# Where the first visit's last two gate/up chunks land, and when the second visit's are fetched

## The chip, the cores and the metric

The kernel runs on one core of a Trainium2 chip. The metric is the device time of one execution in microseconds. The engines are PE (matmuls), DVE, ACT, POOL and SP; SP only issues transfers. Sixteen DMA engines move the data. Transfers issued by SP go through one hardware queue (q1 in the trace), those issued by POOL through another (q0).

## The reference, cut to what matters

One decoder block on 512 tokens of width 1024: a gated DeltaNet group and a convolution group side by side, an output projection with a residual, and then a mixture of experts:

```python
logits = (xt @ w_router + b_router)
top_val, top_idx = lax.top_k(logits, TOP_K)          # 4 of 32 experts
gates = jax.nn.softmax(top_val, axis=-1)
...
hid = x_blk @ w_gate_up[e] + b_gate_up[e]            # 1024 -> 2 x 1024
gate, up = hid[:, :D_FF], hid[:, D_FF:]
gate = jnp.minimum(gate, SWIGLU_LIMIT)
up = jnp.clip(up, -SWIGLU_LIMIT, SWIGLU_LIMIT)
glu = gate * jax.nn.sigmoid(SWIGLU_ALPHA * gate)
return ((up + 1.0) * glu) @ w_down[e] + b_down[e]    # 1024 -> 1024
```

All in float32. Each expert has 8 MB of gate/up weights and 4 MB of down weights, and all 32 are read once.

## The kernel before

The first part (projections, convolutions, the delta rule, output projection) ends with the residual rows `x2`. Then each 128-row tile `t` of four is normed into `xn[:, t % 2, :]`, which lies in `convbuf`, and POOL writes it to `xn_rows` in DRAM (line 543, semaphores `xn_out`). In parallel PE transposes the rows, ACT and DVE copy them as `xnT` into `qkbuf`, and PE forms the logits from it (line 1743, `lgT_done`). Neither buffer is used after that.

The experts are worked through in 32 *visits*, one for each expert, with up to 128 of its tokens in up to four groups of 32. A visit needs:

- its tokens' rows, fetched by POOL with four indirect transfers (*gathers*, line 557) out of `xn_rows` into `wq`. Before the first gather POOL waits for all `xn_out` and for the row numbers (`idx_ready`, made by DVE at line 1352) and copies the numbers (line 552). DVE transposes the rows (`xt_turn`, line 1332, `xt_ready`);
- eight *gate/up chunks* of 1 MB each, one in each slot of `ring`, fetched by SP (line 378, `slot_in[0..7]`);
- four *down chunks* of 1 MB in `dslots` (line 385, `slot_in[8..11]`).

PE's `gate_up(i)` takes the ring slots in pairs (line 1854); after each chunk it raises `gu_used`. Then it runs `down(i - 1)` (line 1890, `d_used`). SP works through one list in order. Visit 0's chunks 0 to 3 are issued after the last projection tile; ring slots 4 to 7 hold the output projection's weights until `op_done` is T, so chunks 4 and 5 follow this, and chunks 6 and 7 also wait for the last normed row:

```python
            for c in range(KC):
                if c == 4:
                    sp.wait_ge(op_done, T)
                if c == 6:
                    sp.wait_ge(xn_ready, T)
                gate_up(0, c)
```

Then come down chunks 0 and 1, a wait for visit 0's gathers, down chunks 2 and 3, a wait for `route_ready`, and visit 1's chunks, each after a wait for `gu_used` of the same slot in visit 0. From visit 2 on a loop issues eight gate/up chunks of visit i and four down chunks of visit i - 1, each when PE has used what the slot held.

Between the router and visit 0, DVE and PE add the experts' gated down biases to `x2` (`routed_bias`, line 1841, and lines 1389 and 1390, `acc_ready`); POOL writes the sums to `acc_rows` (line 590), to which each visit's results are later added by indirect transfers (*scatters*, line 562). PE starts `gate_up(0)` when `xt_ready` is 1 and `acc_ready` is T.

Of the kernel before, what the change touches and what calls it, by code (L numbers as in the profile page):

```python
# [38 lines left out]
def block_kernel(nc, x, attn_norm_w, w_in, gdn_conv_w, gdn_a_log, gdn_dt_bias, gdn_norm_w, cf_dw_w, cf_dw_b,  # L39
                 cf_ln_w, cf_ln_b, w_out, ffn_norm_w, w_router, b_router, w_gate_up, b_gate_up, w_down,  # L40
                 b_down, final_norm_w, out):
    _, SEQ, D = x.shape
# [7 lines left out]
    T = SEQ // P  # L50
    KC = D // P
# [8 lines left out]
    SLOT = 2 * D  # L60
# [10 lines left out]
    with ExitStack() as ctx:  # L71
# [3 lines left out]
        def sem(name):  # L75
            return ctx.enter_context(nc.semaphore(name))


        ring = sb("ring", 8 * SLOT)
# [4 lines left out]
        qkbuf = sb("qkbuf", 2 * 2 * SEQ)  # L84
# [3 lines left out]
        convbuf = sb("convbuf", 2 * (SEQ + CONV - 1) + 2 * SEQ)  # L88
# [14 lines left out]
        def view(t, start, *dims):  # L103
            n = 1
            for d in dims:
                n *= d
            v = t[:, start:start + n]
            names = "abcd"[:len(dims)]
            if len(dims) > 1:
                v = v.rearrange(f"p ({' '.join(names)}) -> p {' '.join(names)}",  # L110
                                **{names[i]: dims[i] for i in range(1, len(dims))})
            return v
# [47 lines left out]
        def take(*dims):  # L160
            n = 1
            for d in dims:
# [53 lines left out]
        finw = rows[:, D:2 * D]  # L216
        fin = view(hbuf, 0, T, D)

        bank = [ctx.enter_context(nc.psum_tensor(f"bank{i}", [P, 512], F32)) for i in range(8)]

        xn_dram = nc.dram_tensor("xn_rows", [NR_ROWS, D], F32, kind="Internal").ap()
# [7 lines left out]
        slot_in = [sem(f"slot_in{i}") for i in range(12)]  # L229
        param_in, gate_in, bias_in, late_in, wr_in = (sem(n) for n in  # L230
                                                      ("param_in", "gate_in", "bias_in", "late_in", "wr_in"))
        fin_in = [sem(f"fin_in{t}") for t in range(T)]
        acc_out, last_out = sem("acc_out"), sem("last_out")
        xn_out = [sem(f"xn_out{i}") for i in range(2)]
# [29 lines left out]
        op_done, x2_ready, rstd2_ready, xn_ready, xn_turned, xnT_ready = (sem(n) for n in (  # L264
            "op_done", "x2_ready", "rstd2_ready", "xn_ready", "xn_turned", "xnT_ready"))
        lgT_done, lgT_copied, lg_done, mx_ready, ex_ready, gate_ready = (sem(n) for n in (
            "lgT_done", "lgT_copied", "lg_done", "mx_ready", "ex_ready", "gate_ready"))
# [82 lines left out]
        @block.sync  # L350
        def _(sp):
            sp.dma_start(xr[:, 0, :], x2d[0:P, :]).then_inc(x_in[0], 16)

            for i, v in enumerate((cf_dw_b, cf_ln_w, cf_ln_b)):
                sp.dma_start(prow[TAPS + i:TAPS + i + 1, :], v).then_inc(param_in, 16)
            sp.dma_start(prow[34:46, :], gdn_conv_w[0].rearrange("w (s c) -> (w s) c", s=3)).then_inc(param_in, 16)
            sp.dma_start(prow[46:48, :], attn_norm_w.rearrange("o (r c) -> (o r) c", r=2)).then_inc(param_in, 16)
            sp.dma_start(prow[48:50, :], ffn_norm_w.rearrange("o (r c) -> (o r) c", r=2)).then_inc(param_in, 16)
            for t in range(1, T):
                sp.dma_start(xr[:, t, :], x2d[t * P:(t + 1) * P, :]).then_inc(x_in[t], 16)  # L360
            for u in range(NU):
                if u >= 8:
                    sp.wait_ge(proj_done, LAST_TILE[u - 8] + 1)
                if u < NU - 2:
                    src = win[:, :, UNITS[u]:UNITS[u] + 256]
                else:
                    c = 4 * (u - NU + 2)
                    src = win[:, c:c + 4, OFF_Z:OFF_Z + QK]
                sp.dma_start(unit_ap(u), src).then_inc(slot_in[u % 8], 16)
            for i in range(4):  # L370
                sp.wait_ge(proj_done, LAST_TILE[4 + i] + 1)
                sp.dma_start(view(ring, (4 + i) * SLOT, 2, D), wout[:, 2 * i:2 * i + 2, :]).then_inc(
                    slot_in[4 + i], 16)

            def gate_up(i, c):
                e = i % E
                src = w_gate_up[0, e].rearrange("(p c) n -> p c n", c=KC)[:, c, :]
                sp.dma_start(view(ring, c * SLOT, SLOT), src).then_inc(slot_in[c], 16)  # L378

            def down_rows(e, u):  # L380
                return w_down[0, e].rearrange("(p c) n -> p c n", c=KC)[:, 2 * u:2 * u + 2, :]

            def down(i, u):
                e = i % E
                sp.dma_start(view(dslots, u * SLOT, 2, D), down_rows(e, u)).then_inc(slot_in[8 + u], 16)

            sp.wait_ge(proj_done, NT)
            for t in range(T):
                sp.dma_start(x2[:, t, :], x2d[t * P:(t + 1) * P, :]).then_inc(xres_in[t], 16)
            for c in range(KC):  # L390
                if c == 4:
                    sp.wait_ge(op_done, T)
                if c == 6:
                    sp.wait_ge(xn_ready, T)
                gate_up(0, c)
            for u in range(4):
                if u == 2:
                    sp.wait_ge(gathered, 16 * GROUPS)
                down(0, u)
            sp.wait_ge(route_ready, 1)  # L400
            m = visits_less_two(sp)
            for c in range(KC):
                sp.wait_ge(gu_used, c + 1)
                gate_up(1, c)
            with sp.Fori(2, m + 2) as i:
                for c in range(KC):
                    sp.wait_ge(gu_used, (i - 1) * KC + c + 1)
                    gate_up(i, c)
                for u in range(4):
                    sp.wait_ge(d_used, (i - 1) * 4 + u + 1)  # L410
                    down(i - 1, u)

            for u in range(4):
                sp.wait_ge(gu_used, m * KC + (KC + 2 * u + 2))
                sp.dma_start(view(ring, u * SLOT, 2, D), down_rows(E - 1, u)).then_inc(slot_in[u], 16)

            sp.wait_ge(scattered, m * (16 * GROUPS) + 32 * GROUPS)
            sp.wait_ge(acc_out, 16 * T)
            for t in range(T):
                sp.dma_start(fin[:, t, :], acc_dram[t * P:(t + 1) * P, :]).then_inc(fin_in[t], 16)  # L420
            for t in range(T):
                sp.wait_ge(fin_ready, t + 1)
                sp.dma_start(out2d[t * P:(t + 1) * P, :], fin[:, t, :]).then_inc(last_out, 16)
            sp.wait_ge(last_out, 16 * T)
# [1047 lines left out]
        def _(pe):  # L1472
# [4 lines left out]
            for j in range(CT):  # L1477
                ins = TR(view(bank[3], 0, CT, 64)[:, j, 0:50], prow[0:50, j * P:(j + 1) * P], ident[0:50, 0:50])
            ins.then_inc(params_turned, 1)
            for t in range(T):  # L1480
# [4 lines left out]
                for c in range(KC):  # L1485
                    ins = TR(bank[c][:, t * P:(t + 1) * P], xr[:, t, c * P:(c + 1) * P], ident)
# [5 lines left out]
            for r in range(2):  # L1492
                for j in range(4):
                    c = 4 * r + j
# [134 lines left out]
            for s in range(NT):  # L1629
                h, steps = gdn_of(s)  # L1630
# [179 lines left out]
            for u in range(T):  # L1810
                ins = M(bank[7][:, 0:E], ones16, Msk[:, u, :], start=(u == 0), stop=(u == T - 1))
# [36 lines left out]
            m = visits_less_two(pe)  # L1848
            pe.sem_inc(d_used, 4)

            def gu_mm(c, g):
                w = view(ring, c * SLOT, 2, D)
                for j in range(4):
                    ins = M(bank[g][GROUP * j:GROUP * (j + 1), :], xT[:, g, c * GROUP:(c + 1) * GROUP],  # L1854
                            w[:, :, j * QD:(j + 1) * QD], start=(c == 0), stop=(c == KC - 1))
                return ins

            def gate_up(i, first=False):

                tokens = tokens_left(pe, i)  # L1860
                for c0 in range(0, KC, 2):
                    pe.wait_ge(slot_in[c0], i * 16 + 48)
                    pe.wait_ge(slot_in[c0 + 1], i * 16 + 48)
                    with pe.If(tokens > 2 * GROUP):
                        for c in (c0, c0 + 1):
                            gu_mm(c, 2)
                        with pe.If(tokens > 3 * GROUP):
                            for c in (c0, c0 + 1):
                                gu_mm(c, 3)
                    for c in (c0, c0 + 1):  # L1870
                        for g in range(2):
                            ins = gu_mm(c, g)
                        ins.then_inc(gu_used, 1)
                    if first and c0 == 0:
                        pe.wait_ge(idx_ready, 1)
                        idx_mm(1, 2 * T + 1)
                    if first and c0 == 6:
                        pe.wait_ge(idx_ready, 2)
                        idx_mm(2, 3 * T + 2)
                    if not first and c0 == 4:  # L1880
                        pe.wait_ge(idx_ready, i + 2)
                        idx_mm((i + 2) % E, (i + 3) * (T + 1) - 1)
# [87 lines left out]
```

## Time and profile before

| | |
|---|---|
| median of 3 runs | 1496.38 us (1495.18 to 1496.44) |
| the profiled execution | 1496.78 us, span 1495.0 us |
| busy: PE, DVE, POOL, ACT | 1285.7, 704.2, 379.5, 202.9 us |
| granted TensorE clock, mean | 0.947 |
| DMA traffic | 451.08 MB, mean 302 GB/s |

The span runs from the first to the last instruction of the core. A busy share is an average over stages, so it does not tell what a change in one stage is worth. In the windows view each line is a stretch: its length, then the busy time of each engine, then the granted clock (1.00 is 2.4 GHz, 0.50 is 1.2 GHz), the share of time for which the 16 DMA engines were busy, and GB/s. In the views of instructions the first two numbers are start and duration in us, SPq stands for an issue by SP, and a bracket gives the engine's idle time before it and what ended it. An arrow reads "written from".

### The profile page before, as it was taken

To read this page: it belongs to the slowest core of one execution; us is meant where nothing else is said; L and a number is where in the kernel's file an instruction comes from. 1 tells how busy PE (TensorE), PEld (TensorE's weight loads), DVE (VectorE), ACT (ScalarE), POOL (GpSimd) and SP (SyncE) were. 2 spreads that over 40 slices of the span, in tenths; PEclk is the share of its full clock that TensorE was granted. 3 is DMA by queue.
4 is the path that set the end of the run, shared out by engine and by line. 5 is a ranking of instruction groups with operands and counts; after the bars stand their busy time and mean duration, and the time that the engine had idled before them with its cause. 6 is when DMAs were issued, how large, how long until landed. Compare 5 with 4: busy or idle time off the path is not lost.

```text
span 1495.0 us, 31945 instructions
## 1 busy us (share of the span) xinstructions
PE 1285.7 (86%) x12386; PEld 563.6 (38%) x12387; DVE 704.2 (47%) x1335; ACT 202.9 (14%) x372; POOL 379.5 (25%) x434
## 2 busy tenths in 40 slices
PE   6997989879878999989989899878888887889982
PEld 3444555555422344333423333323323332233331
DVE  2888888653533345342533325433334443333441
ACT  3123323131300001000100000100000010000012
POOL 4001111020221224322342222333222233222233
PEclk9999999979969999999999999999999999999996
DMA  9221000210368999999999999999999999999984
GB/s 305 67 72 64 1 29 1 112 60 18 117 269 300 391 410 407 403 413 410 411 405 411 409 411 413 408 412 410 409 416 411 409 414 404 401 406 411 410 298 143
DMA packets 93589, 451.08 MB, mean 302 GB/s; under 512 B 18265, under 2 KB 36853, under 8 KB 44375
## 3 DMA queue, kind: packets, MB, share of 16 engines
q1 hardware_dynamic: 70182, 427.88, 70.6%
q0 software_dynamic: 20304, 21.03, 6.1%
q10 hardware_dynamic: 3072, 1.76, 0.5%
q8 instruction: 20, 0.33, 0.1%
q14 instruction: 11, 0.08, 0.0%
HBM read 439.05 MB, written 17.17 MB: 305 GB/s over the span
## 4 chain that ended last, share of the span: by engine, by line
PE 48%; DMA 35%; DVE 10%; issue 3%; ACT 2%; SPq 1%; POOL 1%; POOLq 0%; ACTq 0%; DVEq 0%
DMA ring<-in_w_gate_up_dram 34%; PE bank L1854 24%; PE bank L1890 8%; PE bank L1548 5%; PE bank L1715 4%; DVE dslots L991 2%; DVE qkbuf L1015 1%; PE bank L1614 1%; PE bank L1543 1%; PE bank L1608 1%; DMA xn_rows<-convbuf 1%; DVE vbuf L1015 1%; PE bank L1681 1%; SPq L378 1%; PE bank L1841 0%
## 5 line engine op out<-in xcount | busy, mean ns | idle before, releaser
L1854 PE MATMUL bank<-ring,wq 128*32 128x512 f32 x5184 | 613.8, 626 | 114.2 <-DMA ring<-in_w_gate_up_dram 92.9
L1854 PEld LDWEIGHTS bank<-ring,wq 128*32 128x32 f32 x5184 | 169.2, 114 | 518.2 <-issue 517.8
L1890 PE MATMUL bank<-dslots,intra 128*32 128x256 f32 x5056 | 282.1, 379 | 3.7 <-DMA dslots<-in_w_down_dram 3.4
L1349 DVE TENSOR_REDUCE small<-bank 128x4 f32<-128x8 f32 x34 | 5.7, 167 | 472.7 <-PE bank L1821 472.7
L1890 PEld LDWEIGHTS bank<-dslots,intra 128*32 128x32 f32 x5056 | 166.4, 110 | 127.3 <-issue 28.6
L552 POOL COPY idx_in<-idx 128x4 int32 (+1 forms) x34 | 12.1, 357 | 594.6 <-DVE wq L1332 580.6
L890 ACT ACTIVATE zrows<-intra 128x1024 f32<-128x1024 f32 x32 | 33.8, 1057 | 898.6 <-DVE intra L1429 704.6
L1548 PE MATMUL bank<-hbuf,ring 128*128 128x512 f32 x320 | 147.6, 602 | 0.0
L562 POOL DMA_INDIRECT acc_rows<-rows,idx_out x83 | 133.2, 1605 | 46.5 <-POOL idx_out L552 27.4
L1409 DVE STREAM_TRANSPOSE wq<-bank 128x512 f32<-128x512 f32 x128 | 80.3, 685 | 98.9 <-PE bank L1854 98.9
L557 POOL DMA_INDIRECT wq<-xn_rows,idx_in x88 | 106.9, 1214 | 49.4 <-POOL idx_in L552 29.3
L991 DVE SCALAR_TENSOR_TENSOR dslots<-dslots,small 128x512 f32<-128x512 f32 x120 | 91.8, 765 | 2.7
L1548 PEld LDWEIGHTS bank<-hbuf,ring 128*128 128x128 f32 x320 | 58.7, 194 | 58.4 <-issue 58.4
L1332 DVE STREAM_TRANSPOSE wq<-wq 128x1024 f32<-128x1024 f32 x33 | 67.6, 2047 | 6.7 <-DMA wq<-xn_rows,idx_in 6.7
L569 POOL DMA_DIRECT2D spare<-in_gdn_dt_bias_dram x93 | 68.6, 841 | 0.1
L1715 PE MATMUL bank<-ring,dslots 128*128 128x512 f32 x128 | 59.9, 614 | 2.8 <-DVE dslots L1170 2.8
L884 ACT ACTIVATE rows<-bank,small 128x256 f32<-128x256 f32 x124 | 48.6, 475 | 60.3 <-PE bank L1890 54.9
L1441 DVE SCALAR_TENSOR_TENSOR intra<-zrows,intra 128x1024 f32<-128x1024 f32 x32 | 39.3, 1227 | 22.8 <-PE bank L1890 19.6
L1422 DVE TENSOR_TENSOR zrows<-wq,small 128x256 f32<-128x256 f32 x128 | 45.6, 419 | 0.0
L1323 DVE TENSOR_SCALAR rows<-slot_no,small 128x512 bf16<-128x512 bf16 x140 | 40.1, 350 | 10.1 <-DVE idx L1352 9.6
L1422 DVE TENSOR_TENSOR intra<-wq,small 128x256 f32<-128x256 f32 x128 | 44.5, 409 | 0.0
L491 POOL TENSOR_TENSOR sqbuf<-qkbuf 128x512 f32<-128x512 f32 x8 | 10.4, 1306 | 126.7 <-DVE qkbuf L1033 126.7
(263 smaller groups left out, 897.2 us busy)
## 6 DMA issues: line engine op xcount, KB each, us to landing
ring<-in_w_gate_up_dram SPq DMA_DIRECT2D x256, 1024.0 KB
dslots<-in_w_down_dram SPq DMA_DIRECT2D x124, 1024.0 KB
ring<-in_w_in_dram SPq DMA_DIRECT2D x12, 1024.0 KB
ring<-in_w_out_dram SPq DMA_DIRECT2D x4, 1024.0 KB
ring<-in_w_down_dram SPq DMA_DIRECT2D x4, 1024.0 KB
rows<-in_x_dram SPq DMA_DIRECT2D x4, 512.0 KB, 6.2
hbuf<-in_x_dram SPq DMA_DIRECT2D x4, 512.0 KB, 5.1
xn_rows<-convbuf POOLq DMA_DIRECT2D x4, 512.0 KB, 4.1
```

Of the source, the lines that this page charges most:

```text
L557: pool.indirect_dma_start(out=xg[:, g, :], out_offset=None, in_=xn_q, in_offset=bass.IndirectOffsetOnAxis(ap=idx_in[:, g:g + 1], axis=0), ...
L562: pool.indirect_dma_start(out=acc_q, out_offset=bass.IndirectOffsetOnAxis(ap=idx_out[:, g:g + 1], axis=0), in_=yb[:, g, :], in_offset=None ...
L569: pool.dma_start(spare[0:1, k * H:(k + 1) * H], gdn_dt_bias[0:1, :]).then_inc(done, 16)
L884: ins = A(yb[:, g, :], bank[4 + g // 2][:, (g % 2) * QD:(g % 2 + 1) * QD], ACT.Copy, scale=gates[:, bass.ds(stage * GROUPS + g, 1)])
L991: own.mark(V.scalar_tensor_tensor(out=cacc[:, j, :], in0=ubuf[:, j, k:k + SEQ], scalar=PT[:, j, k:k + 1], in1=cacc[:, j, :], op0=ALU.mult, ...
L1332: V.transpose(xT.rearrange("p g (c s) -> p g c s", c=KC), xg.rearrange("p g (r c) -> p g c r", c=KC)).then_inc(xt_ready, 1)
L1409: V.transpose(hidT[:, g, :, :].rearrange("p h (c s) -> p h c s", c=KC), bank[g][:, :].rearrange("p (h r c) -> p h c r", h=2, c=KC)).then_i ...
L1422: V.tensor_tensor(out[:, g, :].rearrange("p (b s) -> p b s", b=KC), hidT[:, g, half, :].rearrange("p (b s) -> p b s", b=KC), bias.to_broad ...
L1548: ins = M(bank_of(s)[:, :], unit_ap(u)[:, c, half * P:(half + 1) * P], hT[:, c, :], start=(c == 0), stop=(c == KC - 1))
L1715: ins = M(pair[half][:, :], lhs, w, start=(kc == 0), stop=(kc == KC - 1))
L1854: ins = M(bank[g][GROUP * j:GROUP * (j + 1), :], xT[:, g, c * GROUP:(c + 1) * GROUP], w[:, :, j * QD:(j + 1) * QD], start=(c == 0), stop=( ...
L1890: ins = M(b[GROUP * j:GROUP * (j + 1), col:col + QD], actT[:, g, c * GROUP:(c + 1) * GROUP], w[:, cc, j * QD:(j + 1) * QD], start=(c == 0 ...
```

## The change

Visit 0's chunks 6 and 7 no longer go to ring slots 6 and 7. Chunk 6 goes to `qkbuf` after `lgT_done` has reached T, chunk 7 to `convbuf` after all four `xn_rows` writes have landed. SP's waits for the writes stand ahead of chunk 7 and so also ahead of down chunks 0 and 1. Both chunks raise a semaphore of their own, `early_in`. Ring slots 6 and 7 are then free, and SP issues visit 1's chunks 6 and 7 right after `route_ready`, ahead of visit 1's chunks 0 to 5, which wait for `gu_used` as before. PE reads visit 0's chunks 6 and 7 from the two buffers and counts one landing less on `slot_in[6]` and `slot_in[7]`.

```diff
--- before.py
+++ after.py
@@ -216,6 +216,7 @@
         finw = rows[:, D:2 * D]
         fin = view(hbuf, 0, T, D)
 
+        EARLY = {6: view(qkbuf, 0, SLOT), 7: view(convbuf, 0, SLOT)}
         bank = [ctx.enter_context(nc.psum_tensor(f"bank{i}", [P, 512], F32)) for i in range(8)]
 
         xn_dram = nc.dram_tensor("xn_rows", [NR_ROWS, D], F32, kind="Internal").ap()
@@ -229,6 +230,7 @@
         slot_in = [sem(f"slot_in{i}") for i in range(12)]
         param_in, gate_in, bias_in, late_in, wr_in = (sem(n) for n in
                                                       ("param_in", "gate_in", "bias_in", "late_in", "wr_in"))
+        early_in = sem("early_in")
         fin_in = [sem(f"fin_in{t}") for t in range(T)]
         acc_out, last_out = sem("acc_out"), sem("last_out")
         xn_out = [sem(f"xn_out{i}") for i in range(2)]
@@ -372,10 +374,11 @@
                 sp.dma_start(view(ring, (4 + i) * SLOT, 2, D), wout[:, 2 * i:2 * i + 2, :]).then_inc(
                     slot_in[4 + i], 16)
 
-            def gate_up(i, c):
+            def gate_up(i, c, early=None):
                 e = i % E
+                dst, landed_in = (view(ring, c * SLOT, SLOT), slot_in[c]) if early is None else (early, early_in)
                 src = w_gate_up[0, e].rearrange("(p c) n -> p c n", c=KC)[:, c, :]
-                sp.dma_start(view(ring, c * SLOT, SLOT), src).then_inc(slot_in[c], 16)
+                sp.dma_start(dst, src).then_inc(landed_in, 16)
 
             def down_rows(e, u):
                 return w_down[0, e].rearrange("(p c) n -> p c n", c=KC)[:, 2 * u:2 * u + 2, :]
@@ -387,19 +390,24 @@
             sp.wait_ge(proj_done, NT)
             for t in range(T):
                 sp.dma_start(x2[:, t, :], x2d[t * P:(t + 1) * P, :]).then_inc(xres_in[t], 16)
-            for c in range(KC):
+            for c in range(KC - 2):
                 if c == 4:
                     sp.wait_ge(op_done, T)
-                if c == 6:
-                    sp.wait_ge(xn_ready, T)
                 gate_up(0, c)
+            sp.wait_ge(lgT_done, T)
+            gate_up(0, 6, early=EARLY[6])
+            for i in range(2):
+                sp.wait_ge(xn_out[i], 16 * T // 2)
+            gate_up(0, 7, early=EARLY[7])
             for u in range(4):
                 if u == 2:
                     sp.wait_ge(gathered, 16 * GROUPS)
                 down(0, u)
             sp.wait_ge(route_ready, 1)
             m = visits_less_two(sp)
-            for c in range(KC):
+            for c in (6, 7):
+                gate_up(1, c)
+            for c in range(KC - 2):
                 sp.wait_ge(gu_used, c + 1)
                 gate_up(1, c)
             with sp.Fori(2, m + 2) as i:
@@ -1848,8 +1856,8 @@
             m = visits_less_two(pe)
             pe.sem_inc(d_used, 4)
 
-            def gu_mm(c, g):
-                w = view(ring, c * SLOT, 2, D)
+            def gu_mm(c, g, early=False):
+                w = EARLY[c].rearrange("p (h n) -> p h n", h=2) if early else view(ring, c * SLOT, 2, D)
                 for j in range(4):
                     ins = M(bank[g][GROUP * j:GROUP * (j + 1), :], xT[:, g, c * GROUP:(c + 1) * GROUP],
                             w[:, :, j * QD:(j + 1) * QD], start=(c == 0), stop=(c == KC - 1))
@@ -1859,17 +1867,22 @@
 
                 tokens = tokens_left(pe, i)
                 for c0 in range(0, KC, 2):
-                    pe.wait_ge(slot_in[c0], i * 16 + 48)
-                    pe.wait_ge(slot_in[c0 + 1], i * 16 + 48)
+                    early = first and c0 == 6
+                    if early:
+                        pe.wait_ge(early_in, 32)
+                    else:
+                        landed_before = 48 if c0 < 6 else 32
+                        pe.wait_ge(slot_in[c0], i * 16 + landed_before)
+                        pe.wait_ge(slot_in[c0 + 1], i * 16 + landed_before)
                     with pe.If(tokens > 2 * GROUP):
                         for c in (c0, c0 + 1):
-                            gu_mm(c, 2)
+                            gu_mm(c, 2, early)
                         with pe.If(tokens > 3 * GROUP):
                             for c in (c0, c0 + 1):
-                                gu_mm(c, 3)
+                                gu_mm(c, 3, early)
                     for c in (c0, c0 + 1):
                         for g in range(2):
-                            ins = gu_mm(c, g)
+                            ins = gu_mm(c, g, early)
                         ins.then_inc(gu_used, 1)
                     if first and c0 == 0:
                         pe.wait_ge(idx_ready, 1)
```

## Rows read from the trace of the kernel before

**Rows 1.** The page: the chain that ended last, shares of the span by line.
```profile
DMA ring<-in_w_gate_up_dram 34%; PE bank L1854 24%; PE bank L1890 8%; PE bank L1548 5%; PE bank L1715 4%; DVE dslots L991 2%; DVE qkbuf L1015 1%; PE bank L1614 1%; PE bank L1543 1%; PE bank L1608 1%; DMA xn_rows<-convbuf 1%; DVE vbuf L1015 1%; PE bank L1681 1%; SPq L378 1%; PE bank L1841 0%
```

**Rows 2.** Busy time by stretch of the span, with granted clock and DMA share.
```profile
core 0: us, PE busy (x) PEld busy (x) DVE busy (x) ACT busy (x) POOL busy (x), PEclk, DMA share, GB/s
438.00:443.00 5.00, 5.00 (x36) 1.24 (x32) 0.00 (x0) 0.00 (x0) 0.00 (x0) 0.72 0.00 0
466.00:474.70 8.70, 6.94 (x48) 1.94 (x52) 7.06 (x13) 1.06 (x1) 4.38 (x5) 0.68 0.21 67
475.00:620.00 145.00, 141.57 (x1804) 58.12 (x1800) 63.85 (x125) 13.12 (x25) 44.77 (x46) 1.00 1.02 400
620.00:1441.00 821.00, 716.50 (x8472) 276.52 (x8464) 321.00 (x633) 65.59 (x125) 244.90 (x254) 0.96 1.02 408
...
440.00:441.00 1.00, 1.00 (x12) 0.24 (x8) 0.00 (x0) 0.00 (x0) 0.00 (x0) 0.59 0.00 0
...
471.00:472.00 1.00, 1.00 (x12) 0.34 (x8) 0.97 (x2) 0.00 (x0) 0.69 (x2) 0.73 0.36 111
```

**Rows 3.** Timeline of SP's transfer issues: start us, us, line, operation, tiles, count.
```profile
401.05 0.81 SPq L378 DMA_DIRECT2D ring<-in_w_gate_up_dram  x2
...
406.00 0.80 SPq L378 DMA_DIRECT2D ring<-in_w_gate_up_dram  x2
...
423.17 0.80 SPq L385 DMA_DIRECT2D dslots<-in_w_down_dram  x2
...
473.71 0.35 SPq L378 DMA_DIRECT2D ring<-in_w_gate_up_dram  x1
```

**Rows 4.** The chain in order of time, 401 to 475 us: start, us, what.
```profile
406.27 9.41 DMA xn_rows<-convbuf
...
421.07 2.08 DMA wq<-xn_rows,idx_in
...
426.41 7.20 PE bank L1841 x8
...
435.99 7.73 PE bank L1854 x48
...
467.76 7.62 PE bank L1854 x49
```

**Rows 5.** Timeline of instructions: start us, us, engine, line, tiles, [idle before].
```profile
404.43 0.65 PE L1743 MATMUL bank<-qkbuf,small 128*32 128x128 f32 x16 [0.88 <-DVE qkbuf L1308]
...
412.03 0.23 DVE L1352 TENSOR_SCALAR idx<-small,consts 128x4 int32<-128x4 f32 x1
...
392.63 0.57 POOL L543 DMA_DIRECT2D xn_rows<-convbuf  x1
...
415.82 0.26 POOL L552 COPY idx_in<-idx 128x4 int32<-128x4 int32 x1 [4.96 <-DMA xn_rows<-convbuf]
417.05 1.09 POOL L557 DMA_INDIRECT wq<-xn_rows,idx_in  x1 [0.97 <-POOL idx_in L552]
...
445.93 1.07 POOL L557 DMA_INDIRECT wq<-xn_rows,idx_in  x1 [0.86 <-POOL idx_in L552]
...
497.15 1.38 POOL L557 DMA_INDIRECT wq<-xn_rows,idx_in  x1 [0.85 <-POOL idx_in L552]
```

**Rows 6.** POOL's queue (q0), 393.7 to 396 us: packets, MB, share.
```profile
q0 software_dynamic: 144, 0.52, 56.0%
```

**Rows 7.** SP's queue (q1), 407.4 to 410.4 us, nothing on q0.
```profile
q1 hardware_dynamic: 146, 1.04, 102.5%
```

**Rows 8.** Both queues, 410.4 to 415.6 us.
```profile
q1 hardware_dynamic: 219, 1.57, 74.3%
q0 software_dynamic: 144, 0.52, 24.6%
```

**Rows 9.** POOL's queue, 448.4 to 454.6 us.
```profile
q0 software_dynamic: 192, 0.32, 18.4%
```

**Rows 10.** POOL's queue, 497.1 to 501.9 us.
```profile
q0 software_dynamic: 7, 0.03, 1.5%
```

## The prediction

> **What bounds the kernel now.** I read the page's chain first [rows 1]: weight chunks on their way into the ring and the matmuls of line 1854 that eat them share most of the span. A share of the span is not yet a place, so I next cut the span into stages [rows 2]. The reader is to see three things there. From 475 us to 1441 us the DMA engines are full (share 1.02) at 400 to 408 GB/s, so from 475 us on the end is set by when that stream starts, whichever of DMA and PE is ahead in a visit. Before 475 us the stream has two holes: 438 to 443 us (share 0.00) and 466 to 474.7 us (share 0.21, gathers only). At 408 GB/s a chunk of 1024 KB takes 2.57 us.
>
> What ends the second hole? SP's issue at 473.71 us [rows 3], the first gate/up chunk of visit 2, which waits for gu_used: the PE must first have used ring slot 0 in visit 1. At that moment all eight ring slots hold visit 1's chunks and all four dslots hold visit 0's down chunks. So the second hole is lack of a free buffer, and it ends when PE's visit 1 has run for some 6 us (467.76 to 473.71).
>
> So I followed the chain back from there [rows 4]: PE starts visit 1 at 467.76, after visit 0's gate/up, which started at 435.99, after the routed bias (426.41 to 433.6) and its additions, after xt_turn, which starts when visit 0's gathers have landed (421.07 + 2.08 = 423.15), and these were issued after the last xn_rows write had landed: 406.27 + 9.41 = 415.68. Every step in this chain is held by the one before it. Only what moves this chain moves the stream's restart, and with it the end, one for one.
>
> **The change, part by part.**
>
> *Chunk 6 earlier.* It no longer waits for the last normed row (issued at 406.00, second line of [rows 3]) but for the last logits matmul, which ends at 404.43 + 0.65 = 405.08 [rows 5]. The stream gets it 0.9 us earlier; chunks 4 and 5 (issued 401.05) are still moving, so nothing waits for it.
>
> *Chunk 7 and down chunks 0 and 1 later.* They now stand behind the wait for all four xn_rows writes on SP. Before, they were issued in a row right after 406.4. That takes load off the last write. How much is that worth? The third write, alone, was issued at 392.63 [rows 5] and all its 144 packets moved between 393.7 and 396 us [rows 6]: it began 1.1 us after its issue and took 2.3 us at most. The fourth was issued at 406.27, but between 407.4 and 410.4 us only SP's queue moved [rows 7]; its 144 packets came from 410.4 on, mixed with 1.57 MB of SP's, until 415.6 [rows 8]. After the change only chunk 6 is ahead of it. At the latest it begins where it began before, 410.4, and takes 2.3 us: 412.7. At the earliest it behaves as when alone, 406.27 + 3.4 = 409.7. The gathers' other condition bounds the gain: the row numbers (DVE line 1352) are ready at 412.03 + 0.23, and POOL takes them some 0.1 us later, 412.4. POOL's copy therefore moves from 415.82 to between 412.4 and 412.8; I take 3.3 us earlier. The four gathers are then issued from 413.75 to 417.8 instead of 417.05 to 421.07.
>
> *But what do the gathers meet?* The same event that frees POOL frees SP: chunk 7, down 0 and down 1, 3 x 2.57 = 7.7 us of stream, are issued 1 to 2 us ahead of the first gather. Before, the queue was nearly empty when the gathers ran. With nothing in their way they would land 3.3 us earlier, at 419.85; this is the bound of the gain. For gathers beside a running stream there are two places in the trace. Visit 1's four: issued from 445.93 [rows 5], their 192 packets moved between 448.4 and 454.6 [rows 9], so 8.7 us from first issue to last packet. That gives 413.75 + 8.7 = 422.45, 0.7 us earlier than before. Visit 3's, with more of the stream queued ahead: issued from 497.15, and up to 501.9 only 7 packets of their queue had moved [rows 10], a delay of 4.8 us. That gives a start at 418.55; the three chunks end near 413 + 7.7 + 0.9 (the gathers' own bytes) = 421.6; in these 3.05 us, at 192 packets in 6.2 us, 94 packets move, and the other 98 at the lone write's 144 in 2.3 us take 1.6 us: 423.2, no gain. If the rest went on at the loaded rate: 418.55 + 6.2 = 424.75, a loss of 1.6 us. I take 0.7: visit 1's case is the one with just a few chunks issued shortly ahead.
>
> [Rows 7, 10] say that a POOL transfer waits behind what SP has already put in. The Trainium skill (DMA: Bandwidth & Descriptors, section Queues, rings and completion order) has each DMA engine take turns between queues, packet by packet, which would let the gathers in at once; the trace agrees only from 448.4 on in [rows 9], after a delay. By that rule the landing would be near 421 and the time 1494.3; by the rows it is 1495.7.
>
> *Down chunks 2 and 3* follow the gathers, as before (issued 423.17, third line of [rows 3]). PE needs all down chunks only after visit 1's gate/up, which starts at 467.76, and chunk 7 late in visit 0's gate/up, which starts at 435.99 [rows 4]. The delay of some 6 us of chunk 7, down 0 and down 1 is hidden by this.
>
> *Visit 1's chunks 6 and 7* go out right behind down 3, route_ready having long been set, so at about 423 to 424 us instead of at the end of visit 0's gate/up, where PE releases slots 6 and 7. They fill 5.1 us that were in part the first hole. But this only makes the second hole 5.1 us longer: when visit 1's chunk 5 has landed, every buffer is full again, and the next issue still waits for PE in visit 1. Their own price: 2 x 2.57 us more stream beside the four acc_rows writes that POOL issues during the bias additions [rows 4]. These end some us later at worst; POOL asks for them only before visit 2's gathers, which also wait for visit 1's xt_turn, shortly before 467.76. With that cover gone it would be the 5.1 us. SP's two issues (0.33 us each) come while it would wait anyway.
>
> *PE* reads the two chunks from other tiles with the same shapes and counts (visit 0 has the same matmuls, one wait instead of two): nothing.
>
> *The clock* is granted at 0.50 when visit 0's gate/up starts, back to full within 440 to 441 us (0.59 there), so 4.8 us after the stage's start; in visit 1 it is back within 471 to 472 us (0.73), 3.8 us after the start at 467.76 [rows 2, 4]. If it doesn't move with the work, half of the shift is given back (0.35 us); the 1 us between the two places is worth 0.5 us either way.
>
> *Sum:* the write 3.3 us earlier, of which the load on the gathers takes back 2.6; the rest, 0.7 us, is carried by the chain. All of this is read in the execution that took 1496.78 us (span 1495.0); the median of the runs is 1496.38, and I take the difference from it: 1495.7. About 0.2% (3 us) is what a measurement can tell here from no change; so this is within it.
>
> **The rivals.**
>
> *The stream is relieved for good* (forecast if the DMA share were all there is to it): two chunks less after the restart, 5.1 us, 1491.3. For it: the full DMA from 475 on. Against: the second hole, in which no buffer is free. 0.07.
>
> *The gathers are not held up:* landing 419.85, gain 3.3 us, 1493.1. Against: [rows 7, 9, 10], all delayed beside a stream. 0.08.
>
> *They take turns at once:* they start 1.1 us after their issue, 414.85, and take 6.2 us beside the chunks: 421.05, gain 2.1 us, 1494.3. Against: the same rows; for it: here the chunks are issued barely 2 us ahead. 0.14. The rule of the Trainium skill named above is this case.
>
> *The wait moves from the write to the gathers, and is longer:* they wait until all three chunks are through (420.7) and then still need 6.2 us: 426.9, 3.8 us later than before, 1500.2. This is slower from the point where they land after 426.2. For it: [rows 10] with its 4.8 us; against: once the chunks are through, nothing loads them, since down 2 and 3 wait for them. 0.08.
>
> *The write isn't earlier at all*, since what delays it is something other than SP's queue: then both releases stay, but three chunks are added in front of the gathers, about 1 to 2 us later than before. 0.03.
>
> **How the numbers follow.** The likeliest (0.60) is the loaded gather, with ends at 1495 and 1498.0 (start at 418.55 and loaded rate to the end). The range 1493.0 to 1498.0 reaches to the unhindered gathers and leaves out the relieved stream, the long wait and about half of the unhindered case, 0.20. Faster by over 0.2% (under 1493.4): 0.07, half of 0.08, and 0.01 of the rest, 0.12. Slower (over 1499.4): 0.08 and 0.01 of the rest, 0.09. Same: 0.79.
>
> **What the changed profile would show.** The xn_rows write of 406.27 lands near 412 to 412.7 instead of 415.68; POOL's copy starts near 412.5, the gathers near 413.7; xt_turn starts near 422.5. SP issues two gate/up chunks right after down 3. The hole before the restart is longer by about 5 us, and the restart is earlier by as much as xt_turn is. I am wrong in size if xt_turn starts before 421 or after 424.8, and wrong in kind if the restart stays but the end moves, if the second hole is gone, or if PE's visit 1 shows a wait for DMA.

## The result, and the profile after

Slower: the median over 14 runs is 1500.87 us (1498.71 to 1505.46) against 1496.68 us (1494.61 to 1502.68) for 14 runs of the kernel before. The ratio is 1.0031, with a 95% interval of 1.0022 to 1.0040; it is that of the means, which lie 4.6 us apart, while the medians lie 4.2 us apart. The profiled execution took 1499.67 us, its span is 1498.0 us.

The line numbers after the change are 3 to 13 higher: the matmuls of the gate/up chunks are at L1862, the routed bias at L1849, SP's gate/up issue at L381, the gathers at L565, the row numbers' copy at L560. SP's issues of the changed kernel, to be read against [rows 3]:

```profile
403.41 0.80 SPq L381 DMA_DIRECT2D ring<-in_w_gate_up_dram  x2
407.91 0.33 SPq L381 DMA_DIRECT2D qkbuf<-in_w_gate_up_dram  x1
415.89 0.33 SPq L381 DMA_DIRECT2D convbuf<-in_w_gate_up_dram  x1
416.26 11.76 SPq L388 DMA_DIRECT2D dslots<-in_w_down_dram  x4
428.87 50.52 SPq L381 DMA_DIRECT2D ring<-in_w_gate_up_dram  x10
```

The first line is released by the end of the output projection, at 403.41 us, where it was at 401.05 before. This offset of 2.4 us is there before anything of the change has run, so I count from that issue in what follows. The lines show the change at work: chunk 6 goes to qkbuf, chunk 7 to convbuf, 8 us later, when the last xn_rows write has landed, and down 0 and down 1 right behind it. Now the chain [rows 4]:

```profile
408.63 7.18 DMA xn_rows<-convbuf
...
421.16 6.04 DMA wq<-xn_rows,idx_in
...
430.45 7.21 PE bank L1849 x8
...
440.66 7.18 PE bank L1862 x48
...
471.92 8.18 PE bank L1862 x57
```

The write is shorter, 7.18 us instead of 9.41. The last gather, which took 2.08 us to land, now takes 6.04. Counted from SP's first issue the gathers land at 421.16 + 6.04 - 403.41 = 23.79 us; before, at 421.07 + 2.08 - 401.05 = 22.10. That is 1.7 us later, where I had forecast 0.7 us earlier. POOL's instructions [rows 5]:

```profile
408.63 0.56 POOL L551 DMA_DIRECT2D xn_rows<-convbuf  x1 [3.75 <-DVE convbuf L1236]
...
415.94 0.19 POOL L560 COPY idx_in<-idx 128x4 int32<-128x4 int32 x1 [2.20 <-DMA xn_rows<-convbuf]
417.10 1.10 POOL L565 DMA_INDIRECT wq<-xn_rows,idx_in  x1 [0.97 <-POOL idx_in L560]
...
421.16 1.00 POOL L565 DMA_INDIRECT wq<-xn_rows,idx_in  x1 [0.30 <-issue]
```

POOL's copy starts 12.53 us after SP's first issue instead of 14.77, so 2.2 us earlier, and its release is still the write. Traffic by queue, first from the first gather's issue to just before 421.2 us, then to 427 us [rows 9, 10]:

```profile
q1 hardware_dynamic: 205, 1.55, 94.0%
```

...and the second stretch:

```profile
q1 hardware_dynamic: 214, 1.50, 63.3%
q0 software_dynamic: 192, 0.37, 19.8%
```

For 4.1 us after the first gather's issue nothing of POOL's queue moves. Then its 192 packets take up to 5.8 us, and 1.50 MB of the three chunks moves among them. This is the picture of [rows 10] followed by that of [rows 9], and the stream was not through before the gathers were. The windows [rows 2]:

```profile
466.00:475.00 9.00, 3.08 (x16) 0.85 (x20) 8.90 (x18) 1.06 (x1) 2.66 (x4) 0.63 0.06 16
475.00:620.00 145.00, 142.02 (x1812) 58.02 (x1808) 65.42 (x127) 13.03 (x25) 45.71 (x48) 1.00 1.01 392
620.00:1441.00 821.00, 713.17 (x8497) 272.80 (x8490) 319.76 (x626) 64.25 (x125) 247.18 (x255) 0.97 1.02 409
```

From 475 us on nothing has changed in kind. The hole ahead of it is longer (share 0.06 in 466 to 475 us): visit 1's chunks 6 and 7 have been fetched, and SP then waits for a free slot. From PE's start of visit 1 (471.92) to the end of the span are 1026.1 us, before 1027.2.

### The profile page after: what moved, and what is told of

It is laid out like the page before. It is cut to its first block, busy times and chain, and to the rows that moved or that the text cites. A ratio compares the mean times of both kernels' runs of the same rounds, so it can differ in the third digit from the quotient of the medians.

```text
span 1498.0 us, 31976 instructions
## 1 busy us (share of the span) xinstructions
PE 1282.2 (86%) x12386; PEld 560.4 (37%) x12387; DVE 704.8 (47%) x1335; ACT 201.7 (13%) x372; POOL 379.8 (25%) x434
## 4 chain that ended last, share of the span: by engine, by line
PE 44%; DMA 40%; DVE 10%; issue 2%; ACT 2%; POOL 1%; SPq 0%; POOLq 0%; ACTq 0%; DVEq 0%
DMA ring<-in_w_gate_up_dram 38%; PE bank L1862 22%; PE bank L1903 7%; PE bank L1556 5%; PE bank L1723 4%; DVE dslots L999 2%; DVE qkbuf L1023 1%; PE bank L1622 1%; PE bank L1551 1%; PE bank L1689 1%; PE bank L1616 1%; DVE vbuf L1023 1%; PE bank L1849 0%; DMA xn_rows<-convbuf 0%; DVE dslots L1060 0%
## 5 line engine op out<-in xcount | busy, mean ns | idle before, releaser
L1862 PE MATMUL bank<-ring,wq 128*32 128x512 f32 x5136 | 603.7, 621 | 122.2 <-DMA ring<-in_w_gate_up_dram 107.0
L1862 PEld LDWEIGHTS bank<-ring,wq 128*32 128x32 f32 x5136 | 165.6, 114 | 520.2 <-issue 519.6
L560 POOL COPY idx_in<-idx 128x4 int32 (+1 forms) x34 | 12.0, 353 | 595.4 <-DVE wq L1340 584.0
L565 POOL DMA_INDIRECT wq<-xn_rows,idx_in x88 | 107.6, 1223 | 49.4 <-POOL idx_in L560 29.3
L1331 DVE TENSOR_SCALAR rows<-slot_no,small 128x512 bf16<-128x512 bf16 x140 | 40.1, 350 | 10.1 <-DVE idx L1360 9.6
```

Of the source, the lines that this page charges most:

```text
L565: pool.indirect_dma_start(out=xg[:, g, :], out_offset=None, in_=xn_q, in_offset=bass.IndirectOffsetOnAxis(ap=idx_in[:, g:g + 1], axis=0), ...
```

## The experiments

In each, the landing of visit 0's gathers counted from SP's issue at the end of the output projection is the number to look at. Its parts are in a table at the end of this section. Ratios are to the kernel before, with 95% intervals; its runs were taken beside those of the experiments, with a median of 1497.57 us beside x1 to x4 and 1498.22 us beside x5 to x8. x1 to x4 ran on one chip and x5 to x8 on another, each group beside the kernel before on the same chip. Gains and losses in us are worked out from the ratio, which is that of the means. Three theories were stated at the start, G, S and L; the first expectation says what they are.

**x1: SP waits for the gathers ahead of chunk 7.**

```diff
             for i in range(2):
                 sp.wait_ge(xn_out[i], 16 * T // 2)
+            sp.wait_ge(gathered, 16 * GROUPS)
             gate_up(0, 7, early=EARLY[7])
             for u in range(4):
-                if u == 2:
-                    sp.wait_ge(gathered, 16 * GROUPS)
                 down(0, u)
```

> The change, but SP waits for visit 0's gathers before it issues chunk 7, down 0 and down 1. Theory G (the loss is the gathers of visit 0 running beside the three chunks that the same event releases): from the end of the output projection to the gathers' landing it takes about 18.9 us instead of 23.8 (22.1 before), and the time is near 1493.5, 3 us under before. Theory S (visit 1's chunks 6 and 7, issued early, cost time through the acc_rows writes, PE's start of visit 0 or the stream): the gathers land as early, but the time stays 1 to 3 us above that, 1495 to 1497. Theory L (the work before the router is slower in this program by some 2 us, whatever the transfers do): 1495.5, with the output projection ending near 403 us again.

Measured: 1497.06 us, ratio 0.9998 (0.9989 to 1.0008). The loss is gone; the gain of 3 us isn't there. The last gather lands in 2.13 us again, but the write took 8.77 us with only chunk 6 ahead of it, so the gathers landed at 21.5 us, not 18.9. Theory G holds for the gathers; what it said of the write does not.

**x2: the kernel before, chunk 6 with 4 and 5, the rest behind the gathers.**

```diff
-                if c == 6:
-                    sp.wait_ge(xn_ready, T)
+                if c == 7:
+                    sp.wait_ge(gathered, 16 * GROUPS)
                 gate_up(0, c)
             for u in range(4):
-                if u == 2:
-                    sp.wait_ge(gathered, 16 * GROUPS)
                 down(0, u)
```

> The kernel before, with nothing of the change, but chunk 6 is issued with 4 and 5, and chunk 7, down 0 and down 1 wait for visit 0's gathers. Theory G: the last xn_rows write and the gathers both run with little beside them; the gathers land 18.9 us after the end of the output projection and the time is 1493.5. Theory S and L: the same, since nothing of what they name is in it. If it stays at 1496.7, an earlier landing of the gathers isn't handed on to the end and theory G falls too.

Measured: 1495.47 us, ratio 0.9986 (0.9974 to 0.9999). Faster, by 2.1 us. The write took 6.76 us, the gathers landed at 19.4 us. An earlier landing is handed on to the end.

**x3: the change without the early fetch for visit 1.**

```diff
-            for c in (6, 7):
-                gate_up(1, c)
-            for c in range(KC - 2):
+            for c in range(KC):
                 sp.wait_ge(gu_used, c + 1)
                 gate_up(1, c)
```

> The change without its second half: visit 0's chunks 6 and 7 land in the idle buffers, but visit 1's chunks 6 and 7 wait for their turn as before. Theory G: as slow as the change, near 1500.9. Theory S: the 1 to 3 us that it names are gone, 1498 to 1500. Theory L: 1500.9.

Measured: 1501.10 us, ratio 1.0029 (1.0018 to 1.0040), as slow as the change. The early fetch, the half of the change that looks like a gain, neither gives nor takes anything that can be measured. Theory S falls.

**x4: chunk 7 lands in zrows, without a wait for the write.** EARLY[7] is zrows, and the two waits for xn_out are one for rstd2_ready.

```diff
-            for i in range(2):
-                sp.wait_ge(xn_out[i], 16 * T // 2)
+            sp.wait_ge(rstd2_ready, T)
             gate_up(0, 7, early=EARLY[7])
```

> The change, but chunk 7 lands in the idle zrows as soon as the last row's norm is known, so SP doesn't wait for the xn_rows writes and chunk 7, down 0 and down 1 are issued as early as before; visit 1's chunks 6 and 7 still go out early. Theory G: the write is slow again (9 us) and the gathers meet an almost empty queue (landing 2.1 us after the last issue): 1496.7 as before. Theory S: 1 to 3 us above before, 1498 to 1500. Theory L: 1498.7.

Measured: 1498.94 us, ratio 1.0015 (1.0003 to 1.0027). The write is slow (9.99 us) and the gathers quick (2.08 us), as G said; they landed at 22.6 us, 0.5 us later than before, and PE started visit 1 0.3 us later. The time is less clear. G expected no loss; 2.2 us are measured, close to the 2.7 us of the change's second comparison (x7), so this time alone doesn't tell x4 from the change. The fastest executions do: x4's took 1494.67 us and that of before, beside it, 1494.32; the change's stood 4.1 us (1498.71 against 1494.61) and, in x7, 3.8 us (1498.46 against 1494.71) above. What made the other executions of x4 slower isn't shown.

**x5: the kernel before, only chunks 4 and 5 ahead of the write and the gathers.** As x2, with `if c == 6:` in place of `if c == 7:`.

> The kernel before, but only chunks 4 and 5 are issued ahead of the last xn_rows write; chunks 6 and 7 and all four down chunks wait for visit 0's gathers. Theory G, now with its second term (the write is slow while chunk 6 is still under way: it took 6.8 to 8.8 us behind chunk 6 alone): the write lands 3 to 4 us after its issue, POOL then waits for the row numbers instead, and the gathers land 18.8 us after the end of the output projection (22.1 before, 19.4 with chunk 6 ahead), so 0.6 us under the kernel with chunk 6 ahead: about 3 us under before. Rival W (the write is slow here for another reason, not for chunk 6): it still takes 6 us or more, and the gathers land no earlier than 19.4 us.

Measured: 1494.37 us, ratio 0.9980 (0.9968 to 0.9993), 3.0 us faster than before. Its POOL instructions, and the transfer sizes with the time to landing:

```profile
408.79 0.56 POOL L541 DMA_DIRECT2D xn_rows<-convbuf  x1 [3.76 <-DVE convbuf L1226]
...
415.01 0.19 POOL L550 COPY idx_in<-idx 128x4 int32<-128x4 int32 x1 [1.64 <-DVEq L1352]
416.17 1.09 POOL L555 DMA_INDIRECT wq<-xn_rows,idx_in  x1 [0.97 <-POOL idx_in L550]
...
420.19 0.99 POOL L555 DMA_INDIRECT wq<-xn_rows,idx_in  x1 [0.31 <-issue]
```

```profile
xn_rows<-convbuf POOLq DMA_DIRECT2D x1, 512.0 KB, 3.2
```

The write lands in 3.2 us. POOL's wait is now ended by DVE's row numbers (DVEq), no longer by the write, and the gathers land at 420.19 + 2.08 - 403.58 = 18.7 us, where 18.8 was expected. Rival W falls: it was chunk 6. With chunks 4 and 5 alone ahead, 0.43 MB of SP's queue moved in the first us and then the write's 144 packets; the two stretches are 408.8 to 409.8 us and 409.8 to 411.7 us:

```profile
q1 hardware_dynamic: 52, 0.43, 100.4%
```

```profile
q0 software_dynamic: 144, 0.52, 68.6%
q1 hardware_dynamic: 25, 0.07, 9.6%
```

For a lone transfer from POOL the Trainium skill (DMA: Bandwidth & Descriptors, section Anatomy of one DMA — SWDGE (gpsimd) path) gives 2.0 us and the bytes over 436 GB/s, for 512 KB an estimate of 3.2 us; the trace agrees here, and shows 6.8 to 8.8 us as soon as one chunk is still to come ahead of it.

**x6: the change in the same order**, chunks 6 and 7 in the idle buffers, all behind the gathers.

```diff
             sp.wait_ge(lgT_done, T)
-            gate_up(0, 6, early=EARLY[6])
             for i in range(2):
                 sp.wait_ge(xn_out[i], 16 * T // 2)
+            sp.wait_ge(gathered, 16 * GROUPS)
+            gate_up(0, 6, early=EARLY[6])
             gate_up(0, 7, early=EARLY[7])
             for u in range(4):
-                if u == 2:
-                    sp.wait_ge(gathered, 16 * GROUPS)
                 down(0, u)
```

> The change, but only chunks 4 and 5 are ahead of the last write; chunks 6 and 7 in the idle buffers, the four down chunks and visit 1's chunks 6 and 7 all follow visit 0's gathers. Theory G: the same time as the kernel before with this order, within 0.7 us, about 3 us under before. Theory S or L (the early visit 1 chunks or the program itself cost something): 1.5 to 2 us above that kernel, as the two kernels with chunk 6 ahead stood 1.6 us apart.

Measured: 1492.68 us, ratio 0.9973 (0.9962 to 0.9984). Landing at 18.7 us, as in x5. The two differ by 0.0007, inside both intervals. Together they say that neither the idle buffers nor the early fetch cost anything that can be measured once the order of the transfers is right, and that they give nothing that can be told from noise: x6's median is 1.7 us lower, the ratios differ by 1.0 us. S and L fall with this run.

**x7: the change once more.**

> The change itself once more, on the chip of the other three. Theory G: 4 us above before; the output projection ends anywhere from 401 to 404.5 us, as it did in the five profiles so far, so this offset belongs to the single execution and not to the change, and the gathers land 23.5 to 25.5 us after it. Theory L: the output projection ends near 403.4 us in every profile of this program.

Measured: 1499.94 us, ratio 1.0018 (1.0004 to 1.0031). It is slower than before again, by 2.7 us this time against 4.6; the intervals overlap. The output projection ended at 401.37 us here and at 403.41 us in the other execution of the same program, so the offset of 2.4 us in the first profile is the execution's and not the program's: L falls. The chain:

```profile
406.58 8.09 DMA xn_rows<-convbuf
...
414.80 0.20 POOL idx_in L560
...
419.98 6.74 DMA wq<-xn_rows,idx_in
```

The gathers landed at 419.98 + 6.74 - 401.37 = 25.35 us, 3.25 us later than before.

**x8: the change with one chunk ahead of the gathers in place of three.** Down 0 and down 1 wait for them, chunk 7 doesn't.

```diff
             for u in range(4):
-                if u == 2:
+                if u == 0:
                     sp.wait_ge(gathered, 16 * GROUPS)
                 down(0, u)
```

> The change, but down 0 and down 1 wait for visit 0's gathers; of the three chunks that the write's landing releases only chunk 7 is left ahead of them. Theory G as a dose: one chunk ahead holds the gathers for at most 2.6 us instead of 4, and they land 2.1 to 4 us after the last issue instead of 6; the time is 2 to 4 us under the change, near before. Rival H (what matters is that anything at all is released with the gathers, not how much): as slow as the change.

Measured: 1496.34 us, ratio 0.9991 (0.9981 to 1.0002). The last gather lands in 2.12 us: one chunk costs next to nothing (6.2 us from the first gather's issue to the landing, 6.1 with none), three cost 3.8 to 4.7 us (x3, the change and x7). It is issued 1.2 us ahead of the first gather (414.97 and 416.19). From 416.2 to 418.7 us 0.86 MB move on SP's queue and nothing on POOL's, so the gathers do start later, but the last of them is issued only at 420.30 and meets a queue that is nearly empty (0.01 MB from 420 to 421 us). Rival H falls.

| kernel | SP's first issue | write | last gather | landing from first issue | visit 1 starts | median, us | ratio |
|---|---|---|---|---|---|---|---|
| x6 | 401.34 | 3.2 | 2.08 | 18.7 | 63.3 | 1492.68 | 0.9973 |
| x5 | 403.58 | 3.2 | 2.08 | 18.7 | 63.3 | 1494.37 | 0.9980 |
| x2 | 403.48 | 6.76 | 2.12 | 19.4 | 63.6 | 1495.47 | 0.9986 |
| x8 | 401.69 | 7.99 | 2.12 | 20.7 | 64.4 | 1496.34 | 0.9991 |
| x1 | 404.49 | 8.77 | 2.13 | 21.5 | 65.4 | 1497.06 | 0.9998 |
| before | 401.05 | 9.41 | 2.08 | 22.1 | 66.7 | 1496.68 | 1 |
| x4 | 401.69 | 9.99 | 2.08 | 22.6 | 67.0 | 1498.94 | 1.0015 |
| x3 | 403.46 | 8.80 | 5.84 | 25.2 | 69.7 | 1501.10 | 1.0029 |
| the change, again | 401.37 | 8.09 | 6.74 | 25.4 | 70.5 | 1499.94 | 1.0018 |
| the change | 403.41 | 7.18 | 6.04 | 23.8 | 68.5 | 1500.87 | 1.0031 |

All but the last two columns are of one profiled execution each. "Write" and "last gather" run from issue to landing; "visit 1 starts" is PE's first matmul of visit 1, counted from SP's first issue. Over the ten profiles, from there to the end of the span are 1025.0 to 1027.2 us, while the start of visit 1 spreads over 7.2 us: to within 2.2 us a shift is handed on one for one.

## Why the prediction was wrong

The forecast was no measurable change with a gain of 0.7 us; it is a loss of 4.6 us (2.7 in the second comparison). xt_turn started at 427.2 and 426.7 us, past the 424.8 that the prediction had set as a sign of a wrong size.

*The place* was right. The chain, the two holes, the restart that waits for a free slot, and the early fetch that only lengthens the second hole stood as written: x3 and x6 show it. "The stream is relieved for good" did not happen.

*The write, "at the latest it begins where it began before, 410.4, and takes 2.3 us"*: a term that was mis-sized. The bound was 6.4 us from issue to landing; behind chunk 6 alone the write took 6.8 to 8.8 us in six profiles, so POOL's copy came 2.2 us and 1.3 us earlier (12.53 and 13.43 us against 14.77), not 3.3. In the changed kernel the queues moved this, first from 408.63 to 413 us, then to 415.7 us:

```profile
q1 hardware_dynamic: 171, 1.27, 99.3%
```

```profile
q0 software_dynamic: 144, 0.52, 47.4%
q1 hardware_dynamic: 38, 0.18, 16.1%
```

So the write stood still for 4.4 us behind chunk 6, as it did before with more behind it (4.1 us, [rows 8]), against 1.0 us in x5, where 0.43 MB moved in that time. Taking chunk 7 and the down chunks away from behind it spared it the 1.57 MB that moved among its packets [rows 8], but not the wait in front; and the part from there on took 2.8 us here, 3.7 us in x7 and 4.4 us in x1, not 2.3.

*"But what do the gathers meet?"*: this is the step that failed. Two neighbours were at hand, 8.7 us from first issue to last packet with little of the stream ahead, and a start only after 4.8 us with more ahead. I took the first because the chunks are issued "shortly ahead", which is no reason: three chunks are more than the 1.0 MB that moved ahead of visit 1's gathers, from 445.9 to 448.4 us. Measured: no packet for 4.1 us in the change, in x3 and in x7, with 1.4 to 1.6 MB of SP's queue moved in that time, then the two queues together to the end. The three chunks were not through by 421.6 us of my reckoning, which gave them 408 GB/s from their issue: they needed until after 426 us, over 10 us from their issue at 415.89, in part since the two queues together moved only 1.87 MB in 5.8 us from 421.2 us on. First issue to landing is 9.9 to 10.8 us, not 8.7, against 6.1 before. In the change's two profiles the load takes back 4.0 and 4.7 us where the sum had 2.6.

One premise was off without harm: before, the queue was not "nearly empty" when the gathers ran. From 417.05 to 419 us 0.81 MB moved on SP's queue and nothing on POOL's. From first issue to landing it took 6.1 us all the same, as in x5 with nothing ahead.

So of the two terms the gain was 1.3 to 2.2 us instead of 3.3 and the loss 4.0 to 4.7 instead of 2.6: +1.7 and +3.25 us in the two profiles. What happened to the gathers is the worst end of the case that I called likeliest, "start at 418.55 and loaded rate to the end", which stood at a loss of 1.6 us and at the upper end of the range: 4.8 + 6.2 = 11.0 us from first issue to last packet by its numbers, 10.1 and 10.8 us to the landing as measured. The write's smaller gain and the 0.6 us below come on top of that. The rival "the wait moves from the write to the gathers, and is longer" (0.08) had the direction and nearly the size, 3.8 us, but not the mechanism: the gathers didn't wait until all three chunks were through, they moved beside the second half of them.

*The rule of turns at once* is wrong here: only after 4.1 us of one queue alone do the two move side by side. The trace agrees with the rule of the Trainium skill (the page and section named in the prediction) only for the second part.

*A term that I didn't have:* from the end of the last bias addition to the first matmul of visit 0 took 1.06 us before and 1.68 and 1.89 us in the two executions of the change. From xt_turn's start to that matmul are 12.8 to 12.9 us in seven profiles, and 13.3 to 13.6 in x4 and the two of the change. Why isn't known, and no run here was aimed at it. In the first profile visit 0's gate/up then went faster, its first stretch of matmuls in 7.18 us instead of 7.73; the clock was back 3.7 us after its start instead of 4.8, as these windows show (0.50, then 0.81 for the slice in which it rose):

```profile
443.00:444.00 1.00, 1.00 (x8) 0.20 (x4) 0.00 (x0) 0.00 (x0) 0.00 (x0) 0.50 1.03 422
444.00:445.00 1.00, 1.00 (x12) 0.33 (x8) 0.00 (x0) 0.00 (x0) 0.00 (x0) 0.81 0.29 115
```

That stretch takes 6.7 to 7.7 us over the ten profiles, so it can't be put down to the change. Together 1.7 + 0.6 - 0.5 = 1.8 us later at the start of visit 1.

*What stays open.* The two comparisons of the change give 1.0031 and 1.0018; the two profiles put the start of visit 1 1.8 and 3.8 us later than before, in the other order. So the landing varies from execution to execution, one profile gives it only to about 1.5 us, and the loss in time is accounted for in direction and rough size, not to the microsecond. Why a transfer of POOL's stands still behind SP's chunks isn't shown either; that it does is.

## What to carry to other kernels

Look at what one event releases. Here the wait in front of three bulk transfers was the same as that in front of small transfers on the critical path, and the small ones lost 3.8 to 4.7 us. Put the bulk behind the small ones if its consumer is late; here three lines of order in the kernel before (x5) gave 3 us, and the new buffers gave nothing measurable of their own. A buffer freed early is worth something only if the hole it fills is the one that ends last.

## What the runs showed of the hardware

A transfer issued by POOL didn't share the DMA engines at once with what SP had already issued: the gathers stood 4.1 us behind three chunks, and at 497 us 4.8 us with 7 of their packets moved. Behind one chunk, issued 1.2 us before the first gather, none of their packets moved for 2.5 us, and the last gather landed as fast as with none ahead (x8).

A 512 KB write moved no packet for 4.1 us or more wherever chunk 6 was ahead of it (eight profiles), and for 1.0 us with only chunks 4 and 5 ahead, of which 0.43 MB moved in that time (x5, x6). It landed in 3.2 us there, in 6.8 to 8.8 us behind chunk 6 alone, and in 9.4 and 10.0 us with more chunks behind it as well.

The start of the expert part shifts by 2.0 us between two executions of the same program (401.37 and 403.41), and by 3.4 us (401.05 to 404.49) over the ten profiles, whose work up to there is the same.
